# Strassen operand without the inverse root in a two-block transformer kernel on Trainium2: quarters split straight into their homes, GpSimd scales the gate by the root

## The reference, cut to what matters

```python
def _rmsnorm(x, g):
    xf = x.astype(jnp.float32)
    y = xf * lax.rsqrt(jnp.mean(xf * xf, axis=-1, keepdims=True) + EPS)
    return (y * g.astype(jnp.float32)).astype(x.dtype)

def _swiglu(h, w_gu, w_down):
    g, u = jnp.split(h @ w_gu, 2, axis=-1)
    return (jax.nn.silu(g) * u) @ w_down

x = x + 0.5 * _swiglu(_rmsnorm(x, norm_ffn1), w_ffn1_gu, w_ffn1_down)
```

## Time and profile before

| | us |
|---|---|
| median of 3 runs | 3402.6 (3398.45 to 3403.41) |
| the profiled execution | 3403.3 |
| its span, first to last instruction | 3401.5 |
| PE busy | 3233.7 (95%) |
| DVE / POOL / ACT busy | 1794.5 / 1592.5 / 1122.8 |
| mean granted TensorE clock | 0.984 |

### The profile page before, as it was taken

One profiled execution on the slowest core, in us unless ns is written; L12 is line 12 of the kernel. 1 busy time (PEld: TensorE's weight loads), 2 busy tenths in 40 slices (PEclk: granted clock), 3 DMA queues, 4 the chain that ended last, 5 costly groups with the idle time before them and its releaser, 6 DMA issues.

```text
span 3401.5 us, 47654 instructions
## 1 busy us (share of the span) xinstructions
PE 3233.7 (95%) x18771; PEld 1658.9 (49%) x19068; DVE 1794.5 (53%) x2985; ACT 1122.8 (33%) x2094; POOL 1592.5 (47%) x1100
## 2 busy tenths in 40 slices
PE   8999998999999759999999999999999996999999
PEld 4555653655654324444445554555554442444444
DVE  4365558146547876664113376666566686656100
ACT  1434422234332423231002445555554423323000
POOL 4555752445664234443333556555564433444332
PEclk9999999999999979999999999999999997999999
DMA  3122112112121201112222011111112211111312
GB/s 130 40 52 61 58 56 102 41 48 66 37 80 39 98 26 63 52 61 96 70 70 90 29 58 52 49 51 52 52 35 93 85 62 38 62 50 50 103 50 83
DMA packets 59278, 211.72 MB, mean 62 GB/s; under 512 B 7345, under 2 KB 7729, under 8 KB 58545
## 3 DMA queue, kind: packets, MB, share of 16 engines
q1 hardware_dynamic: 54304, 191.34, 17.3%
q10 hardware_dynamic: 4752, 17.30, 1.3%
HBM read 181.36 MB, written 20.97 MB: 59 GB/s over the span
## 4 chain that ended last, share of the span: by engine, by line
PE 89%; DVE 7%; issue 2%; ACT 2%; POOL 1%; DMA 0%; DVEq 0%; ACTq 0%; POOLq 0%
PE pair L1179 26%; PE pair L1177 25%; PE pair L1178 23%; PE pair L1397 3%; PE pair L1366 3%; DVE arena L2159 2%; PE pair L1378 2%; PE pair L1621 1%; PE pair L1647 1%; PE pair L1632 1%; DVE residual L2159 1%; DVE residual L2162 1%; PE pair L1575 1%; PE pair L1197 1%; DVE operand L2159 1%
## 5 line engine op out<-in xcount | busy, mean ns | idle before, releaser
L959 POOL TENSOR_SCALAR panel_parts<-panel_raw 128x1024 f16<-128x1024 f32 (+3 forms) x204 | 209.1, 1025 | 928.8 <-issue 655.7
L1177 PE MATMUL pair<-operand,panel_parts 128*128 128x512 f16 x1536 | 586.6, 382 | 23.9 <-DVE operand L2159 11.0
L1177 PE MATMUL pair<-arena,panel_parts 128*128 128x512 f16 (+1 forms) x1520 | 575.0, 378 | 27.5 <-DVE arena L2159 18.9
L1179 PE MATMUL pair<-operand,panel_parts 128*128 128x512 f16 x1536 | 584.2, 380 | 7.5
L1179 PE MATMUL pair<-arena,panel_parts 128*128 128x512 f16 (+1 forms) x1520 | 573.9, 378 | 5.5
L1178 PE MATMUL pair<-arena,panel_parts 128*128 128x512 bf16 (+1 forms) x1415 | 534.3, 378 | 0.0
L1178 PE MATMUL pair<-operand,panel_parts 128*128 128x512 bf16 x1393 | 530.5, 381 | 0.0
L960 POOL TENSOR_TENSOR panel_parts<-panel_raw,panel_parts 128x1024 bf16<-128x1024 f32 (+3 forms) x204 | 466.5, 2287 | 17.0
L996 POOL TENSOR_SCALAR arena<-arena,row_inv 128x256 f32<-128x256 f32 (+7 forms) x256 | 343.6, 1354 | 236.4 <-DVE row_inv L2225 236.1
L2162 DVE SCALAR_TENSOR_TENSOR residual<-pair,residual 128x1024 f32<-128x1024 f32 (+1 forms) x64 | 61.3, 958 | 422.7 <-PE pair L1179 394.6
L1132 POOL TENSOR_SCALAR arena<-arena,row_inv 128x384 f32<-128x384 f32 (+1 forms) x128 | 188.6, 1484 | 161.6 <-DVE row_inv L2846 161.6
(11 more groups left out here) (296 smaller groups left out, 5747.8 us busy)
## 6 DMA issues: line engine op xcount, KB each, us to landing
panel_raw<-in_wl SPq DMA_DIRECT2D x58, 512.0 KB, 3.5
panel_raw<-in_wm SPq DMA_DIRECT2D x56, 512.0 KB, 3.5
ffn_extra<-in_wgu SPq DMA_DIRECT2D x18, 1024.0 KB, 4.9
panel_raw<-in_wgu SPq DMA_DIRECT2D x18, 1024.0 KB, 5.0
panel_raw<-in_wdn SPq DMA_DIRECT2D x32, 512.0 KB, 3.5
residual<-residual_spill SPq DMA_DIRECT2D x31, 512.0 KB, 6.9
residual_spill<-residual ACTq DMA_DIRECT2D x24, 512.0 KB, 2.6
panel_raw<-in_wgu SPq DMA_DIRECT2D x16, 512.0 KB, 3.6
```

Source lines behind the costliest of these rows:

```text
L959: chained(nc.gpsimd.tensor_scalar(hi[:, c], RAW[:, s, c], HI_MAX, -HI_MAX, ALU.min, ALU.max))
L1177: nc.tensor.matmul(out, stat[0], mov[0], start=first, stop=False, skip_group_check=skip)
L1179: return nc.tensor.matmul(out, stat[1], mov[0], start=False, stop=last, skip_group_check=skip)
```

## The change

It keeps the root out of the operand of Strassen's scheme, as the plain tiles do already, and puts it in after the products.

- `norm_operand` on DVE goes. ACT multiplies `XT` by the gain alone, in place, ahead of its root function (8 copies with a scale).
- The plain tiles' splits are written straight into the places that four of the seven operands have (`HOMES`, in `XP`): Q11, Q12, Q21 and Q22 without the root. `PLAIN` goes. Three operands (Q11, Q22, Q21 as they are) then need no copy, clip and subtraction of their own. Four are left: `B_T1`, `B_T3` (split by DVE), `B_T2`, `B_T4` (low part by POOL). `B_T4` takes Q12's place, once the last plain tile is done.
- The order of the operand stage changes: the four differences directly behind pair 0; pair 1; weight sums; the splits; five clips; pairs 2 and 3; two clips; the clip of `B_T4`.
- In each block the gate has two new DVE steps (3 and 5: bank times `ROOT` into `SILH`), silu works in place on `SILH`, and POOL multiplies the silu by `ROOT` (`silu_root`). There are nine steps in place of seven. `silu_root(b, 0)` stands in POOL's program ahead of the last two `weight_rest` of block b+1, `silu_root(b, 1)` behind them. The clips 5 and 6 of block b+1 stand on DVE behind step 5.

```diff
+        HOMES = [(XPF[:, 4096 * c:4096 * c + 2048], XPF[:, 4096 * c + 2048:4096 * c + 4096].bitcast(LO)) for c in range(4)]
+        B_T1, B_T2, B_T3 = [parts(22528 + 2048 * c, 2048) for c in range(3)]
+        B_T4 = B12
+        OPERANDS = [B11, B_T2, B_T1, B_T3, B21, B22, B_T4]
...
   POOL, ffn:
-                for i in range(5):
+                term_rest(B_T2, Q22, 0)
+                for i in range(7):
                     weight_rest(0, i)
-                term_rest(1, Q22, 0)
-                term_rest(2, Q11, 1)
-                for i in range(5, 7):
-                    weight_rest(0, i)
-                for b in range(1, BLOCKS):
-                    for i in range(7):
-                        weight_rest(b, i)
+                term_rest(B_T4, Q21, 1)
+                def silu_root(b, h):
+                    pool.wait_ge(half_silu, 2 * block_of(idx, b) + h + 1)
+                    nc.gpsimd.tensor_tensor(SILH[h], SILH[h], ROOT[:, h * HALF:(h + 1) * HALF], ALU.mult).then_inc(silu_scaled, 1)
+                for b in range(BLOCKS):
+                    if b + 1 < BLOCKS:
+                        for i in range(5):
+                            weight_rest(b + 1, i)
+                    silu_root(b, 0)
+                    if b + 1 < BLOCKS:
+                        for i in range(5, 7):
+                            weight_rest(b + 1, i)
+                    silu_root(b, 1)
...
   ACT, ffn:
+                act.wait_ge(ffn_spilled, 16 * KT * idx)
+                for k in range(KT):
+                    nc.scalar.activation(tview(XT, k), tview(XT, k), ACT.Copy,
+                                         scale=SC[:, 16 * (idx - 1) + k:16 * (idx - 1) + k + 1]).then_inc(normed, 1)
                 inverse_root(SILP[0], ROOT, f"rms{idx}", 0, 3)
...
                 plain_silu(0)
-                for i in range(5):
+                weight_part(0, 0)
+                for home, q, n in ((B_T1, Q11, 9), (B_T3, Q12, 10), (B_T2, Q22, 11)):
+                    term_part(home, q, n)
+                plain_silu(1)
+                for i in range(1, 5):
                     weight_part(0, i)
-                plain_silu(1)
-                for c, q, n in ((0, Q11, 8), (5, Q22, 8), (1, Q22, 11), (2, Q11, 9), (3, Q12, 10), (4, Q21, 8)):
-                    term_part(c, q, n)
...
+                act.wait_ge(tile_ready[3], tiles_before(f"gu{idx}", PLAIN_F // 2, 3))
+                term_part(B_T4, Q21, 12)
...
   DVE, evict(b, step):
+                    elif step == 3:
+                        dve.wait_ge(product_done, 7 * g + 5)
+                        m = tt(SILH[0], b1, ROOT[:, 0:HALF], ALU.mult)
...
+                    elif step == 5:
                         dve.wait_ge(evicted, n + 5)
+                        m = tt(SILH[1], b3, ROOT[:, HALF:T], ALU.mult)
...
+                    elif step == 7:
+                        dve.wait_ge(evicted, n + 7)
+                        dve.wait_ge(silu_scaled, 2 * g + 1)
                         m = tt(FACT[:, 0:HALF], b2, SILH[0], ALU.mult)
                     else:
-                        dve.wait_ge(half_silu, 2 * block_of(idx, b) + 2)
+                        dve.wait_ge(silu_scaled, 2 * g + 2)
                         m = tt(FACT[:, HALF:T], b4, SILH[1], ALU.mult)
...
   DVE, ffn:
                 plain_pair(0)
-                norm_operand()
+                term_sum(Q11, Q12, Q11, 9, 8)
+                term_sum(Q12, Q22, Q12, 10, 9)
+                term_sum(Q22, Q22, Q11, 11, 10)
+                term_sum(Q21, Q21, Q22, 12, 11)
+                plain_pair(1)
                 for n in range(4):
                     weight_sum(0, n)
-                plain_pair(1)
+                term_split(B_T1, Q11, 1)
+                term_clip(B_T2, 3).then_inc(term_clipped, 1)
+                term_split(B_T3, Q12, 2)
                 for i in range(5):
                     weight_clip(0, i)
...
+                for f in range(2, PLAIN_F):
+                    plain_pair(f)
                 for i in range(5, 7):
                     weight_clip(0, i)
+                term_clip(B_T4, 4).then_inc(term_clipped, 1)
...
-                    evict(b, 3)
+                    for step in (3, 4, 5):
+                        evict(b, step)
                     if more:
                         weight_clip(b + 1, 5)
                         weight_clip(b + 1, 6)
```

More of the change, by code:

```diff
@@ L595, in build @@
         half_silu = sem("half_silu")
+        silu_scaled = sem("silu_scaled")
         normed = sem("operand_normed")
@@ L764, in weight_source, with operand_at @@
             return (a11, s2, s1, s3, a12, s4, a22)[i]
+        def operand_at(k, c):
+            home, t = HOMES[2 * (k // 4) + c // HALF], slice(k % 4 * HALF, (k % 4 + 1) * HALF)
+            return home[0][:, t], home[1][:, t]
         def block_banks(b):
@@ L1509, in block @@
                         pe.wait_ge(weight_lo, 7 * n + i + 1)
-                        if b == 0:
-                            if i in (1, 2):
-                                pe.wait_ge(term_ready_pool, 2 * (idx - 1) + i)
-                            else:
-                                pe.wait_ge(term_ready, 5 * (idx - 1) + {0: 1, 3: 3, 4: 4, 5: 4, 6: 5}[i])
-                        if i < 3:
-                            if b < 2:
-                                for j in (2 * b, 2 * b + 1):
-                                    pe.wait_ge(tile_taken[j], tiles_before(f"gu{idx}", turn, j))
-                            elif i == 1:
-                                pe.wait_ge(evicted, 7 * (n - 2) + 7)
-                            else:
-                                pe.wait_ge(half_silu, 2 * (n - 2) + (1 if i == 0 else 2))
+                        if b == 0 and i in (1, 6):
+                            pe.wait_ge(term_ready_pool, 2 * (idx - 1) + (1 if i == 1 else 2))
+                        if b == 0 and i in (2, 3):
+                            pe.wait_ge(term_ready, 2 * (idx - 1) + i - 1)
+                        if i < 3 and b < 2:
+                            for j in (2 * b, 2 * b + 1):
+                                pe.wait_ge(tile_taken[j], tiles_before(f"gu{idx}", turn, j))
+                        elif i < 3:
+                            pe.wait_ge(evicted, 9 * (n - 2) + (4, 8, 6)[i])
                         if i == 3:
-                            pe.wait_ge(evicted, 7 * n + 1)
+                            pe.wait_ge(evicted, 9 * n + 1)
                         if i == 4:
@@ L1533, in block @@
                             w, t = slice(k * P, (k + 1) * P), slice(k * HALF, (k + 1) * HALF)
-                            m = product(banks[bank], (hi[:, w], lo[:, w]), (TCH[i][:, t], TCL[i][:, t]),
+                            m = product(banks[bank], (hi[:, w], lo[:, w]), (OPERANDS[i][0][:, t], OPERANDS[i][1][:, t]),
                                         first and k == 0, k == 3, True)
@@ L2336, in split_gained @@
                 else:
-                    split(PLAIN[k][0], PLAIN[k][1], GAINED[k % 2], x_split)
+                    a, c = k // 4 * 2, k % 4 * HALF
+                    hi, lo = (XPQ[:, a:a + 2, s_, c:c + HALF] for s_ in range(2))
+                    split(hi, lo.bitcast(LO), GAINED[k % 2].rearrange("p (a c) -> p a c", a=2), x_split)
             def sum_square(l, k):
@@ L2575, in plain_pair, with term_sum, term_clip, term_split @@
                     split(AP_[0][:, t], AP_[1][:, t], AFP[j], act_split)
[L2577 to L2595 removed]
+                def term_sum(out, a, b, n, after):
+                    dve.wait_ge(normed, 12 * (idx - 1) + after)
+                    tt(out, a, b, ALU.subtract).then_inc(normed, 1)
+                def term_clip(home, n):
+                    dve.wait_ge(term_hi, 4 * (idx - 1) + n)
+                    return V_.tensor_scalar(home[0], home[0], HI_MAX, -HI_MAX, ALU.min, ALU.max)
+                def term_split(home, q, n):
+                    hi, lo = [v.rearrange("p (k t) -> p k t", k=4) for v in home]
+                    chained(term_clip(home, n))
+                    tt(lo, q, hi, ALU.subtract).then_inc(term_ready, 1)
                 def weight_sum(b, n):
@@ L2616, in evict @@
                 def evict(b, step):
-                    n = 7 * block_of(idx, b)
+                    g = block_of(idx, b)
+                    n = 9 * g
                     b1, b2, b3, b4 = block_banks(b)
@@ L2645, in keep_block @@
                 def keep_block(b):
-                    for step in (4, 5, 6):
+                    for step in (6, 7, 8):
                         evict(b, step)
-                    dve.wait_ge(evicted, 7 * block_of(idx, b) + 7)
+                    dve.wait_ge(evicted, 9 * block_of(idx, b) + 9)
                     t = slice((PLAIN_F + b) * T, (PLAIN_F + b + 1) * T)
```

100 lines of the change are left out of this document (28 added, 72 removed).

## The result

The changed kernel takes 3414.7 us (median of 6 runs, 3413.5 to 3416.8) against 3402.1 us for the kernel before (6 runs on the same chip, 3398.5 to 3403.4): a ratio of 1.0036, 95% interval 1.0026 to 1.0047. It is 12.5 us slower, and 5.7 us above the forecast of 3409. The profiled execution took 3414.07 us (span 3412.2), 10.8 above the 3403.3 of before.

A forecast was written before the change was run, and what follows sets the result against it. PE, busy 3233.7 of 3401.5 us, was taken as the bound. 3403.3 - 41 (operand stage) + 37 (blocks) + 10 (down projection) = 3409.3, given as 3409; the 8-in-10 range was 3375 to 3428.

The forecast's parts named there:

- operand stage: Stretch before the Strassen blocks: DVE's shorter program starts block 1 20.4 us earlier per FFN, 41 us in two.
- blocks 1 to 16, each: Last eviction waits for POOL's second silu product, so product 4 starts late: 1.15 us a block, bounds 0.9 and 1.5.
- blocks, both FFNs: The wait in 32 blocks of two FFNs: +37 us, bounds 29 and 48.
- down projection: After block 17: POOL splits the first down panel later, PE waits 5 us; +10 us in all, bounds 9 and 17.
- pair 1: Operand stage, DVE: 6.8 us, and about 2 for its silu on ACT and a panel split, bounds 0 to 3.
- The wait of 4.07 us beside POOL's subtraction: Operand stage: DVE waits for POOL's whole term_rest of 4.07 us, taken once, bounds 0 and 4.07.
- slack of 0.16 us: In a block before the change: 0.16 us to spare between step 0's end on DVE and PE's product 4.
- The estimate that two more evictions fit: In the blocks: DVE, 186 of 308 us busy, has room for 34 x 0.7 x 2 us more.
- A: Rival, in the blocks: POOL's silu product is hidden and adds nothing; 3372 us, faster, chance 0.15.
- B: Rival, operand stage: DVE and POOL hardly wait for each other, gain 30 us an FFN; 3390 us, chance 0.12.
- C: Rival, between blocks: POOL's three instructions are slowed, wait 2.1 us a block, 66 us in all; 3438 us, chance 0.12.
- D: Rival, in the blocks: each wait brings the low clock level, 32 x 2.6 us more; 3490 us, chance 0.03.

The follow-up runs named there:

- experiment 3: Changed kernel without the two silu-by-root products on POOL, DVE's last two evictions waiting for ACT's silu instead: 3363.7 us, 0.9888 of the kernel before.
- experiment 8: Changed kernel with ACT making the operand copies and pair 1's silu ahead of block 0's first weight copy: 3407.8 us, 1.0014 of the kernel before.
- experiment 9: Changed kernel with eight unused 128x1024 products added on DVE between pair 0 and the four differences: 3430.9 us, 1.0082 of the kernel before.
- experiment 1: Changed kernel with silu_root(b, 1) on POOL ahead of the last two weight subtractions instead of behind them: 3398.2 us, 0.9999 of the kernel before.
- experiment 7: Changed kernel with the low part of B_T2 made by DVE instead of POOL: 3411.2 us, 1.003 of the kernel before.
- experiment 4: Changed kernel with the first two down panels split on POOL ahead of block 17's two silu products: 3397.0 us, 0.9991 of the kernel before.
- experiment 5: Changed kernel with all weight copies, clips 3 to 6 and POOL's subtractions made earlier, both silu products behind them: 3373.6 us, 0.9925 of the kernel before.
- experiment 6: Changed kernel with pair 3 and its silu moved behind block 0's weight sums, step 0 and three clips: 3406.0 us, 1.0015 of the kernel before.
- experiment 2: Changed kernel with silu_root(b, 0) also moved behind the last two weight subtractions on POOL: 3451.5 us, 1.0147 of the kernel before.
- experiment 10: Changed kernel with the edits of experiment 4, experiment 5 and experiment 6 together: 3355.8 us, 0.9869 of the kernel before.

## Why the prediction was right

The forecast was "slower, by an amount at the edge", as a small difference of two large terms; 3409 was given and 3414.7 came. Step by step:

| step | predicted | measured | from |
|---|---|---|---|
| operand stage, both FFNs | -41 | -39.5 by the timeline, -38.4 by experiment 3 | end of plain work to block 1: 58.1 and 57.4 before, 38.8 and 37.2 after |
| blocks 1 to 16, each | +1.15 | +1.14 | 19.28 against 18.14 |
| blocks, both FFNs | +37 | +36.5 | 32 x 1.14 |
| down projection, both FFNs | +10 | +13.9 | idles 4.34, then 14 and 11 slow matmuls |
| sum | +6 | +10.9 by the terms, +10.8 profiled | |

**Operand stage.** The mechanism held: DVE's program shorter by the norm's work, and port waits beside POOL that give a part back. The steps lay within 2 us: block 0 at 1228.18 where 1225.3 was written (with 0.85 us by which this execution ran later from the start, 1226.2), product 4 at 1248.15 for 1247.2. That they lie so close is in part luck, since terms within them missed both ways: the four differences took 12.55 us for 14.0, pair 1 took 12.96 for 8.8, and from the end of pair 3 to product 4 it was 10.2 for 11.1. Pair 1 was long by ACT's silu (a wait of 4.92 us), which experiment 8 traced to the copy that waits for a DMA, and by 2.4 us beside a panel split (experiment 9); the prediction had about 2 for both. It had looked at what stands ahead of the silu on ACT, and not at what that work itself waits for. The wait of 4.07 us beside POOL's subtraction, counted whole and once, was 3.75 (2.29 to 6.04). A second one, the weight sum of 4.42 us in place of 0.69 at 1241.65 beside `term_rest(B_T4)`, is in the prediction only as a later start of the sums.

The Trainium skill, "SBUF — State Buffer", section "SBUF: two separate sides", calls the shared port pair an exclusive lock and not a split of bandwidth. The traces agree: DVE instructions between SBUF tiles that met a POOL subtraction ended their own undisturbed length, less 0.14 or 0.15 us, behind POOL's end. The clip of 0.69 us did so at 1412.24 for 1411.70 (experiment 1), the subtraction of 2.29 us at 1220.58 for 1218.43 and the weight sum of 0.69 us at 1246.07 for 1245.53 (changed kernel). POOL's subtraction stayed at 1.16 us in experiment 1; where one began 0.53 us before the end of a DVE clip (at 1213.98, experiment 7) it took 4.45 us for 4.07, so it too waited.

**Blocks.** This is the step that decided the sign, and it was read from one block of the trace of before: slack of 0.16 us, a product on POOL due behind two subtractions, seen by DVE at 2.83 us into the next block. The product took 1.26 to 1.27 us for the 1.20 taken (bounds 1.16 and 1.76), DVE's wait was 1.21, the period 19.28. (The estimate that two more evictions fit set both FFNs' 34 x 0.7 x 2 us against the 308 us of one FFN; with one FFN's half of it they fit all the more, and DVE's busy time there rose from 186 to 201 us.)

**Down projection: the term that was mis-sized.** The prediction put an idle of 4.3 us there, and 4.34 came; it took 5 in all and no low level, because an idle of 3.28 us had left the matmul at 0.38. One row of 3.28 was made to speak for 4.3. The level did fall, in both FFNs, and 3.0 and 2.3 us were lost behind it. The upper bound of 17 held.

**The rivals.** A (the product is hidden) fell: DVE waits for it, and starts at 2.83 us where A needed 1.7. Experiment 1 put the product early enough for A, and the slack still didn't hold, because the subtraction then stood beside DVE's clip. B (hardly any waits between DVE and POOL in the operand stage) fell by the 6.04 and 4.42 us rows. C (POOL's instructions between the blocks slowed) fell: 1.16 and 1.26 beside DVE's evictions from PSUM. D (a low level in every block) fell: no matmul of blocks 1 to 17 took over 0.39 us.

**Left open.** DVE reached its first difference in FFN 1 at 1182.12 us in the changed kernel, 1180.13 in experiment 4, 1178.90 in experiment 1 and 1177.69 in experiment 5, though all run the same instructions up to there; why isn't known, and differences of a few us between two kernels are safe only where rows place them. Why the level of the clock fell behind some idles of 2 to 4 us and not behind others isn't settled either (below).

## What to carry to other kernels

When work moves to another engine, its length is the smaller question: find its place in that engine's queue, follow the value to the instruction that waits for it, and hold the delay against the slack there (0.16 us here); here 1.14 us once in a block took back 36.5 of the 39.5 us that the shortened stage gave. Before giving a move up, reorder: the same instructions in another order took some 40 us off (experiment 5), and with the other edits 72, but each reorder was worth its gain only once the instruction newly late behind it, or newly beside a POOL instruction on the port, had been looked up too. Take a stall's length from the queue, and for the clock behind it don't let one row of a shorter stall speak.

## What the runs showed of the hardware

**The clock behind idles of 2 to 4 us.** All idles told of here followed matmuls at the high level (0.38 us, 0.216 from start to start). Behind every one of 4.20 us and more, slow matmuls followed, 6 to 14 of them at 0.43 us from start to start, so 1.3 to 3 us a time; over two such stretches of the changed kernel (1248.15 to 1253.20 and 1592.25 to 1598.18 us) the granted clock is 0.50, the lower level. Between 2.2 and 3.9 us it went either way: it stayed high behind 3.26 us (experiment 9), and started low behind 2.73 us (experiment 8). At one place of FFN 2, ended by POOL's panel split and 3.27 to 3.29 us long in all fourteen kernels, nine stayed high all through, as here the changed one:

```profile
2712.81 0.38 PE L1193 MATMUL pair<-arena 128*128 128x512 f16 x1 [3.29 <-POOL panel_parts L968]
```

two started low, as here experiment 6, and three fell 1.1 to 1.6 us behind the restart:

```profile
2706.27 0.58 PE L1193 MATMUL pair<-arena 128*128 128x512 f16 x1 [3.28 <-POOL panel_parts L968]
```

And the level can fall a little behind the idle, while PE works again. Of experiment 2's 32 idles of 2.2 us ahead of product 4 one did so (the second row is the first of its eight slow matmuls; those between took 0.38):

```profile
2977.91 0.38 PE L1193 MATMUL pair<-arena,panel_parts 128*128 128x512 f16 x1 [2.22 <-DVE residual L2167]
...
2979.20 0.59 PE L1193 MATMUL pair<-arena,panel_parts 128*128 128x512 f16 x1
```

So the length of an idle doesn't tell alone, and neither does the first matmul behind it: the rows of the next 2 us have to be read too, which the prediction didn't do with its idle of 3.28 us (there they are at 0.38 as well).

**Which DVE work waits beside POOL.** Beside a POOL subtraction, DVE's products out of PSUM kept their 0.69 us; a weight sum with two SBUF inputs went from 0.69 to 4.42, and a one-input clip from f32 to f16 from 0.69 to 1.57. A 0.28 us clip of 512 columns, f16 to f16, took 1.26 us (experiment 10). I had counted the large operands alone as at risk. POOL's product of 512 columns with f32 output took 1.26 us, its subtraction of the same size with bf16 output 1.16.
